# The third blocks of heads 4 and 5 taken as one couple by seven products, in a two-layer encoder step

## What is computed

```python
z = h @ w_in                                  # columns: B | C | xin | c_q | c_kv | k_rope | gate_conv | gate_mla
yc, new_buf = short_conv(c_g * xin, conv_buf, conv_w)
y_a = b_g * yc
y_b = mla_attention(q_nope, q_pe, q_pos, ckv_all, kpe_all, k_pos, w_uk, w_uv)
merged = sigmoid(ga) * y_a + sigmoid(gb) * y_b
x = x + rmsnorm(merged @ w_o, g_post_mix)
```

## Time and profile before

| what | us |
| --- | --- |
| median of 3 runs | 1710.92 (1710.36 to 1710.96) |
| the profiled execution | 1711.26 |
| its span, first to last instruction | 1709.5 |
| TensorE busy | 1698.6 (99%) |
| VectorE busy | 1324.2 (77%) |
| ScalarE busy | 868.9 (51%) |
| GpSimd busy | 106.2 (6%) |

### The profile page before, as it was taken

How to read it: one execution, slowest core, us unless ns; L and a number is a source line. 1 busy time by engine, 2 the same in 40 slices (tenths; PEclk the granted TensorE clock), 3 DMA queues, 4 the chain that set the end, 5 groups by cost and what they waited for, 6 DMA issues and landing times.

```text
span 1709.5 us, 31894 instructions
## 1 busy us (share of the span) xinstructions
PE 1698.6 (99%) x12687; PEld 1685.4 (99%) x12687; DVE 1324.2 (77%) x2538; ACT 868.9 (51%) x1681; POOL 106.2 (6%) x143
## 2 busy tenths in 40 slices
PE   9999999999999999999999999999999999999997
PEld 9999999999999999999999999999999999999997
DVE  7778877878788777668688788777878887777665
ACT  7636454555554545446366374545545536444452
POOL 1311211000000000000002221000000000000000
PEclk9999999999999999999999999999999999999998
DMA  7889989454321322233138898444623313322231
GB/s 249 219 199 215 252 222 241 125 175 155 112 74 51 112 87 87 87 99 99 62 121 221 209 232 217 133 140 114 201 106 99 99 54 98 97 88 87 74 99 56
DMA packets 94133, 233.64 MB, mean 137 GB/s; under 512 B 9888, under 2 KB 21408, under 8 KB 93984
## 3 DMA queue, kind: packets, MB, share of 16 engines
q1 hardware_dynamic: 72352, 179.16, 32.9%
q0 software_dynamic: 20352, 50.34, 14.6%
q10 hardware_dynamic: 1280, 2.10, 0.3%
HBM read 221.20 MB, written 60.69 MB: 165 GB/s over the span
## 4 chain that ended last, share of the span: by engine, by line
PE 99%; DVE 1%; ACT 0%; issue 0%; DVEq 0%
PE ring L820 20%; PE ring L822 20%; PE ring L821 20%; PE att L820 12%; PE att L822 11%; PE att L821 11%; PE att L3680 1%; PE att L815 1%; PE att L814 1%; PE att L827 0%; PE ring L3516 0%; PE att L3496 0%; PE att L828 0%; PE att L3843 0%; ACT rope_s L1289 0%; PE att L3503 0%
## 5 line engine op out<-in xcount | busy, mean ns | idle before, releaser
L820 PE MATMUL ring<-xs_hi,w_lo 128*128 128x288 f32 x1792 | 532.8, 297 | 0.6 <-issue 0.4
L822 PE MATMUL ring<-xs_hi,w_hi 128*128 128x288 f32 x1792 | 527.9, 295 | 0.0
L821 PE MATMUL ring<-xs_lo,w_hi 128*128 128x288 f32 x1792 | 527.7, 294 | 0.0
L2133 DVE TENSOR_TENSOR w_lo<-w_raw,w_hi 128x1024 fp32r<-128x1024 f32 (+1 forms) x370 | 377.1, 1038 | 27.7 <-ACT w_hi L1218 19.0
L820 PEld LDWEIGHTS ring<-xs_hi,w_lo 128*128 128x128 f32 x1792 | 336.6, 188 | 2.9 <-issue 1.2
L821 PEld LDWEIGHTS ring<-xs_lo,w_hi 128*128 128x128 f32 x1792 | 336.8, 188 | 1.3
L822 PEld LDWEIGHTS ring<-xs_hi,w_hi 128*128 128x128 f32 x1792 | 336.6, 188 | 0.0
L822 PE MATMUL att<-f_hi,w_hi 128*128 128x288 f32 x960 | 283.2, 295 | 0.0
L821 PE MATMUL att<-f_lo,w_hi 128*128 128x288 f32 x960 | 282.9, 295 | 0.0
L820 PE MATMUL att<-f_hi,w_lo 128*128 128x288 f32 x960 | 282.6, 294 | 0.0
L820 PEld LDWEIGHTS att<-f_hi,w_lo 128*128 128x128 f32 x960 | 180.4, 188 | 0.0
(11 more groups left out here) (355 smaller groups left out, 3215.5 us busy)
## 6 DMA issues: line engine op xcount, KB each, us to landing
w_raw<-blocks_in SPq DMA_DIRECT2D x189, 512.0 KB, 3.7
weight_sums<-blocks_in POOLq DMA_DIRECT2D x72, 512.0 KB, 7.0
w_raw<-weight_sums SPq DMA_DIRECT2D x96, 256.0 KB, 4.4
w_raw<-blocks_in SPq DMA_DIRECT2D x70, 256.0 KB, 4.2
weight_sums<-weight_sums POOLq DMA_DIRECT2D x48, 256.0 KB, 6.7
small_raw<-small_in SPq DMA_DIRECT2D x16, 320.0 KB, 5.0
small_raw<-small_in SPq DMA_DIRECT2D x32, 128.0 KB, 5.2
my_kept<-rx SPq DMA_DIRECT2D x12, 288.0 KB, 6.1
```

Of the source, the lines that this page charges most:

```text
L820: pe.matmul(out, w[1], x[0], start=first, stop=False)
L821: pe.matmul(out, w[0], x[1], start=False, stop=False)
L822: return pe.matmul(out, w[0], x[0], start=False, stop=last)
L2133: return dve.tensor_tensor(out, a, hi.bitcast(F32), ALU.subtract)
```

## The change

Heads 4 and 5 become one unit with 18 positions (`UNITS`, `UNIT_HALVES`). Their third blocks form a new couple `c=2` (n = 18 to 24) by seven products: head 4 does products 18, 19, 20, 23 and 24, head 5 does 21 and 22. Head 4 thus has 19 products of 12 matmuls and head 5 has 16, where each had 14 and a direct block of 48 matmuls. What head 4 leaves for head 5 is kept in a new tile `block_kept` and in half of the cosine table's tile (`block_fifth`), which SP loads again afterwards (`cos_back`).

A layer has 13 couples of weight sums, in the order (2,0), (2,1), (3,0), (3,1), (4,0), (4,2), (4,1), (5,0), ... as (head, couple). There are 60 positions: head 2 at 10, head 3 at 18, the unit of heads 4 and 5 at 26, head 6 at 44, head 7 at 52. The extra slot is used at positions 33, 39, 45, 51 and 57 instead of eight times from 15 on. `pos_before` and SP's loop are unchanged. Position 33 is the eighth of the unit and holds products 11 and 12 of head 4, the first sums of head 4's couple 1. The last position of the unit is half full, and its high and low parts are made at half width. New orders of work for heads 4 and 5 are written out for all engines.

```diff
-N_EXTRA = 8
+PAIRED = (4,)
+N_EXTRA, EXTRA_FIRST = 5, 33
...
+    if is_first(head):
+        MIXED_ORDER[head] = [0, 1, 18, 19, 2, 3, 4, 5, 6, 20, 23, 24, 9, 10, 11, 12, 13, 14, 15] \
+            if head == FIRST_MIXED else [0, 1, 2, 3, 4, 5, 6, 18, 19, 20, 23, 24, 9, 10, 11, 12, 13, 14, 15]
+    elif is_second(head):
+        MIXED_ORDER[head] = [0, 1, 2, 3, 4, 5, 6, 21, 22, 9, 10, 11, 12, 13, 14, 15]
...
-EXTRA, EXTRA_AT = 8, tuple(range(HEAD_POS[FIRST_MIXED] + N_HEAD, POSITIONS, N_HEAD + 1))[0:N_EXTRA]
+EXTRA, EXTRA_AT = 8, tuple(range(EXTRA_FIRST, POSITIONS, N_HEAD + 1))[0:N_EXTRA]
...
+SUM_ORDER = [(head, c) for head in range(FIRST_MIXED, LAST_MIXED + 1)
+             for c in ((0, 2, 1) if is_first(head) else (0, 1))]
+LAYER_SUMS = len(SUM_ORDER)
...
-                begun = 2 if h == FIRST_MIXED else 1
-                second = 4 if h == LAST_MIXED else 5
-                if j in (begun, second):
-                    sp.wait_ge(pl.sums_third, 16 * (head_sums(L, h, j // second) + 1))
+                for h, n in pieces:
+                    if n % 9 == 2 or n == 21:
+                        sp.wait_ge(pl.sums_third, 16 * (head_sums(L, h, n // 9) + 1))
...
+                    if is_first(h) and j == 15:
+                        sp.wait_ge(pl.kept_read, L * len(PAIRED) + PAIRED.index(h) + 1)
+                        sp.dma_start(pl.cos[:, 0:NH], tables[0][:, 0:NH]).then_inc(pl.cos_back, 16)
...
+                if is_first(h):
+                    for i in (0, 1, 2, 5):
+                        product(h, 2, i)
+                    turns(h)
+                    product(h, 2, 6)
+                    product(h, 1, 0)
+                    product(h, 1, 1)
+                    attended(h)
+                    for i in range(2, 7):
+                        product(h, 1, i)
+                    return
+                if is_second(h):
+                    product(h, 2, 3)
+                    product(h, 2, 4)
+                    product(h, 1, 0)
+                    product(h, 1, 1)
+                    turns(h)
+                    for i in range(2, 5):
+                        product(h, 1, i)
+                    attended(h)
+                    product(h, 1, 5)
+                    product(h, 1, 6)
+                    return
```

More of the change, by code:

```diff
@@ L90, in is_mixed, with is_first, is_second @@
     return FIRST_MIXED <= h <= LAST_MIXED
-N_EXTRA = 8
-HEAD_POS = [0]
+PAIRED = (4,)
+N_EXTRA, EXTRA_FIRST = 5, 33
+def is_first(h):
+    return h in PAIRED
+def is_second(h):
+    return h - 1 in PAIRED
+MIXED_ORDER = {}
+for head in range(FIRST_MIXED, LAST_MIXED + 1):
+    if is_first(head):
[3 more added lines that the diff above has]
+        MIXED_ORDER[head] = [0, 1, 2, 3, 4, 5, 6, 21, 22, 9, 10, 11, 12, 13, 14, 15]
+    elif head == FIRST_MIXED:
+        MIXED_ORDER[head] = [0, 1, 7, 8, 2, 3, 4, 5, 6, 9, 10, 11, 12, 13, 14, 15]
+    elif head == LAST_MIXED:
+        MIXED_ORDER[head] = [0, 1, 2, 3, 4, 5, 6, 9, 10, 11, 12, 13, 14, 7, 8, 15]
+    else:
+        MIXED_ORDER[head] = list(range(16))
@@ new lines @@
+UNITS = [(head, head + 1) if is_first(head) else (head,) for head in range(HEADS) if not is_second(head)]
+UNIT_HALVES = {unit: [(head, n) for head in unit if is_mixed(head) for n in MIXED_ORDER[head]] for unit in UNITS}
+HEAD_POS, HALF_AT, UNIT_OF, UNIT_POS = {}, {}, {}, {}
+POSITIONS = 0
+for unit in UNITS:
+    UNIT_POS[unit] = (len(UNIT_HALVES[unit]) + 1) // 2 if is_mixed(unit[0]) else N_HEAD
+    for head in unit:
+        HEAD_POS[head], UNIT_OF[head] = POSITIONS, unit
+        HALF_AT[head] = 0 if head == unit[0] else len(MIXED_ORDER[unit[0]])
+    POSITIONS += UNIT_POS[unit]
@@ new lines, with position, whole_block, n_loads @@
+assert len(EXTRA_AT) == N_EXTRA and (POSITIONS - N_EXTRA) % N_HEAD == 0
+def position(q):
+    head = max(h for h in range(HEADS) if HEAD_POS[h] <= q)
+    unit = UNIT_OF[head]
+    j = q - HEAD_POS[head]
+    return unit, UNIT_HALVES[unit][2 * j:2 * j + 2] if is_mixed(head) else None
+def whole_block(pieces):
+    return len(pieces) == 2 and pieces[0][0] == pieces[1][0] and (pieces[0][1], pieces[1][1]) in ((0, 1), (7, 8), (9, 10))
+def n_loads(q):
+    if q >= POSITIONS or not is_mixed(position(q)[0][0]):
+        return 1
+    return 1 if whole_block(position(q)[1]) else len(position(q)[1])
@@ L103, with pos_width @@
+def pos_width(q):
+    if q >= POSITIONS or not is_mixed(position(q)[0][0]):
+        return 1024
+    return 512 * len(position(q)[1])
 NBW = NBC + POSITIONS - N_HEAD * HEADS
@@ L134, in weight_loads @@
     for q in range(POSITIONS + N_HEAD):
-        two = any(is_mixed(h) and HEAD_POS[h] + (2 if h == FIRST_MIXED else 1) <= q < HEAD_POS[h + 1]
-                  for h in range(HEADS))
-        uses[pos_slot(q)] += 2 if two else 1
+        uses[pos_slot(q)] += n_loads(q)
         use_of["pos", q] = uses[pos_slot(q)]
@@ L934, in sum_of, with weight_of @@
                 return pl.sums[head_sums(L, h, c)][:, SUM_ROWS[k], :]
[L936 to L948, removed]
+            def weight_of(h, n):
+                if n in (7, 8):
+                    return half_of(h, 4, n - 7)
+                c, i = divmod(n, 9)
+                first = h - 1 if c == 2 and is_second(h) else h
+                one, two = (((h, 2), (h, 3)), ((h, 0), (h, 1)), ((first, 4), (first + 1, 4)))[c]
+                if i < 2:
+                    return half_of(*one, i)
+                return half_of(*two, 1) if i == 4 else sum_of(h, c, (2, 3, 5, 6).index(i))
             def pos_load(q):
@@ new lines, in block_rest, with block_right, kept_sum @@
+                def block_rest():
+                    own_freed(23)
+                    own.step(dve.tensor_tensor(pl.ga[:, cols(1)], pl.block_kept[:, :], pl.block_fifth, ALU.subtract))
+                def block_right():
+                    src = ready(24)
+                    own.wait()
+                    dve.tensor_tensor(pl.ga[:, cols(1)], pl.ga[:, cols(1)], src, ALU.add).then_inc(pl.ring_free, 1)
+                def kept_sum():
+                    src = ready(21)
+                    dve.tensor_tensor(pl.block_kept[:, :], pl.block_kept[:, :], src, ALU.add).then_inc(pl.ring_free, 1)
```

330 lines of the change are left out of this document (288 added, 42 removed).

## The result

The changed kernel takes 1746.89 us in the median (1731.16 to 1749.75, 6 runs), the kernel before 1710.69 (1710.31 to 1710.96, 6 runs): a ratio of 1.0196, 95% interval 1.0178 to 1.0214. That is 36.2 us more, where 28 more were forecast, and inside the stated range. The runs of before lie within 0.7 us, those of the changed kernel within 18.6. The profiled execution took 1742.01 us with a span of 1740.2, so it is 30.8 us longer than the profiled execution of before and 5 us short of its own median.

What follows compares the result with a forecast made beforehand. The prediction took TensorE, busy 99% of the span, as the bound: 1711.26 - 3.2 + 23.3 + 5.8 + 1.5 + 1.0 = 1739.7 us profiled, median 1739. Range for 8 in 10: 1725 to 1751.

Steps and rivals of the forecast that it cites:

- The 24 matmuls, -3.2 us: Each layer's direct third blocks become seven products, 12 matmuls less a layer at 0.133 us each: 3.2 us less in all.
- Heads 4 and 5, 0: VectorE and ScalarE have room for the new work in heads 4 and 5, closest margin 0.9 us: no cost.
- SP held at position 9 until the seventh couple: SP reaches position 33's load after position 9 and waits for sums, holding later loads; up to 45 us in layer 0.
- The release, 183.5 us in layer 0: Layer 0's seventh couple is made and SP goes on at 183.5 us, bounds 181 to 188.5.
- the small effect: With SP silent, a GpSimd turn of the sums shortens only from 17.4 to 15.5 us; release 5 us earlier.
- the rival in which the turn shrinks toward 10 us: Couples come much sooner with SP silent; layer 0 loses about 10 us, layer 1 none or 2: 1720 us, 5%.
- The release in layer 1, 1010.5 us: Layer 1's seventh couple is made and SP goes on at 1010.5 us, bounds 1009 to 1012.4.
- Release to low part, 10.5 us: Position 15 lands 8 us after release, its high and low parts take 2.5 us: 10.5 us, bounds 8 to 13.5.
- The second wait, up to 6.5 us after the low part: Head 2's turns wait for probabilities, ready 6.5 us after position 15's low part; the two products between take 3.2 us.
- The sum for each layer: Delay of head 2's turns: 23.3 us in layer 0 (18 to 31), 5.8 us in layer 1 (2 to 11).
- the 1 us for positions 16 to 19: Late landings of positions 16 to 19 and small weights: 1 us in layer 0, 0.5 in layer 1, bounds 0 and 3.
- The clock, 1 us: After some 20 us idle TensorE runs slow, mostly covered by the second wait: 1 us more, bounds 0 to 3.

Runs made afterwards that it cites:

- the late first load: Changed kernel, but position 33's load is issued when position 27 is done instead of position 9: 1707.94 us, ratio 0.9984 to the kernel before.
- one slot less: Kernel before, with the extra slot first used at position 45 and its first load issued when position 39 is done: 1710.86 us, ratio 1.0002.
- the three other profiles: Changed kernel unedited again (1740.47 us), with 150 idle matmuls in layer 0 (1741.42 us), and with 33 in layer 1 (1743.0 us).
- the wait alone, in the kernel before: Kernel before, with SP also waiting for the layer's seventh couple of weight sums in front of position 15's load: 1743.93 us, ratio 1.0196.
- the run with 150 matmuls: Changed kernel with 150 extra matmuls before product 10 of head 2 in layer 0, keeping TensorE busy through the stall: 1741.42 us, ratio 1.0179.
- two pairs: Late-first-load kernel with heads 2 and 3 also paired: 1710.37 us; with product 18's copy and product 19's step moved earlier in head 2: 1709.28 us.

## Why the prediction was right, step by step

- *The 24 matmuls, -3.2 us.* Right. From head 4's turns to head 6's it is 81.7 us (281.91 to 363.57) against 83.2 before, 1.6 us a layer, and the kernel with the late first load gains 2.8 us.
- *Heads 4 and 5, 0; five slots in heads 2 and 3, 0; the thirteenth couple, 0.* Right: in the profile of the changed kernel there is no wait of TensorE there, and the runs with the late first load and with one slot less agree.
- *SP held at position 9 until the seventh couple.* Right, in both layers, and shown from both sides: taking it away gives 1707.9, adding it to the kernel before gives 1743.9.
- *The release, 183.5 us in layer 0 (turns of 15.5 us with SP silent).* Right in this execution: 182.3, turns of 15.5 and 15.4. That it is so close is partly luck: the three other profiles have 180.9, 177.3 and 176.3, all below the bound of 181. The trace speaks for the small effect and against the rival in which the turn shrinks toward 10 us. That the queues take turns in the engines may well hold (the Trainium skill, "DMA: Bandwidth & Descriptors", SWDGE vs HWDGE vs iDMA); no run here shows it. With SP silent the software queue alone holds 73.4% of the 16 engines over a turn of 15.5 us, and that each accumulation waits for the one before is the likely reason why the turn isn't shorter; no run took that dependence away.
- *The release in layer 1, 1010.5 us.* Too late, outside its bounds. Counted from head 1's turns it was to come after 39.7 us (1010.5 - 970.8), with 38.2 as the lower bound, and came after 34.4 (1030.39 - 996.00). SP was silent for 17 us and not for 23. The four profiles have 34.4, 34.8, 38.1 and 40.9, so one value couldn't be right for all.
- *Release to low part, 10.5 us.* Too small, and beyond its own bound of 13.5: TensorE goes on 14.8 us after the release in layer 0 (182.28 to 197.09) and 15.4 in layer 1 (1030.39 to 1045.76). I took the landing time of a burst that TensorE's pace spreads over 13 us; here SP issues 14 loads and stores in 10 us, and 256 KB take 11.5 us to land, not 6.8. Without position 33's halves in front (the wait alone, in the kernel before) the low part was done 7.1 us after the release.
- *The second wait, up to 6.5 us after the low part.* Right: 6.5 and 6.2 us. It hung by little: the exponents stand behind position 16's high part, which began at 198.4, half a microsecond before the row maxima were done. With the wait alone position 16 came last, and this stretch was 10.7 and 11.0 us.
- *The sum for each layer.* The delay of head 2's turns was 26.9 us in layer 0 (77.9 against 51.0 from head 1) where 24.3 were summed, with the 1 us for positions 16 to 19, and 5.1 in layer 1 (55.8 against 50.7) where 6.3 were. Layer 1 comes near by luck: a release 5.3 us early and a landing 4.9 us slow nearly cancel. In the profile of the run with 150 matmuls, whose release in layer 1 came after 38.1 us, the delay there is 9.8 us.
- *The clock, 1 us.* Nearly right in size, wrong in place, so its size is luck. In layer 0, where I looked for it, the low clock is covered by the second wait, and the 1 us added for it isn't there. In layer 1 it costs 1.6 us after two short waits, which I hadn't thought of.

The sum of the parts is -3.2 + 26.9 + 5.1 + 1.6 = 30.4 us against 30.8 measured in the profiled execution. The median lies 5 us above that execution. That part isn't explained term by term. It belongs to the spread, which the prediction gave only as bounds of the release and didn't name as a result: a kernel that never waits for the sums doesn't show how much their turns vary.

## What to carry to other kernels

A load with a wait in an in-order queue has to be placed by the later of two things, when its slot is free and when its data are there, and what it costs is told by what stands behind it. A resource that is used for the first time needs a look of its own: the rule "load when the last user is done" has no last user, and the value put in for it was right only for the load that used to be first. After such a stall the backlog lands slower than a burst that is spread over time (11.5 us in the median against 6.8 in the earlier trace rows), and the place in it counts: the position wanted first landed 5 us after the release when it stood at the head of the burst, and 12.3 us after it behind 0.8 MB of others. A term that comes out near its forecast in one execution isn't confirmed by that alone: here the release alone moved by 6 us from one execution to the next.

## What the runs showed that I had not expected

- Two waits of 2.2 and 2.6 us, with 3.2 us of work between them, came before a fall of the clock to 0.50: the ten transposes behind them took 2.39 us in place of 1.25. With two pairs a single wait of 1.9 us came before such a fall in layer 0, and one as long in layer 1 did not. A wait of 24 us cost nothing through the clock, because the second wait behind it was long enough to cover the slow work. With the wait alone in the kernel before, TensorE stood for another 4.8 and 7.4 us and came out slow: 2.4 and 1.6 us lost up to head 3's turns.
- A program in which nothing waits for the accumulating DMAs repeats within about 2 us (the kernel before, 1709.61 to 1711.68 in 21 runs); with SP waiting for the seventh couple, the changed kernel's times spread over 19 us.
- In the kernel before the seventh couple is made 45 us after position 9 is done (188 against 143), and no wait in its trace shows that, since nothing asks for this couple so early.
